# The first chunk of a decoder block, unit by unit: x and w_in interleaved, meta tokens loaded once, zeros multiplied before x lands

## What is computed

```python
u = rmsnorm(h, norm_attn_pre[l])          # h: [pad | 16 meta tokens | 256 rows of x]
z = u @ w_in[l]                           # w_in: (2048, 8448)
qa, ka, va, qb, kb, vb, ga, gb = jnp.split(z, SPLITS, axis=-1)
...
mix = jax.nn.sigmoid(ga) * (ya @ w_branch_a[l]) + jax.nn.sigmoid(gb) * (yb @ w_branch_b[l])
h = h + rmsnorm(mix @ w_out[l], norm_attn_post[l])
u = rmsnorm(h, norm_ff_pre[l])
f = jnp.square(jax.nn.relu(u @ w_ff1[l])) @ w_ff2[l]
h = h + rmsnorm(f, norm_ff_post[l])
```

## Time and profile before

| | |
|---|---|
| median of 3 runs | 1377.43 us (1377.38 to 1377.56) |
| profiled execution, its own time | 1377.66 us |
| its span, first to last instruction | 1375.9 us |
| PE busy (matmul) | 1356.5 us, 99% of the span |
| PE weight loads (beside the matmuls) | 1111.6 us, 81% |
| DVE busy | 759.3 us, 55% |
| ACT busy | 627.4 us, 46% |
| POOL busy | 51.5 us, 4% |
| first product of chunk 1 | starts at 36.79 us |

### The profile page before, as it was taken

How to read it: one execution, slowest core, us unless ns; L and a number is a source line. 1 busy time by engine, 2 the same in 40 slices (tenths; PEclk the granted TensorE clock), 3 DMA queues, 4 the chain that set the end, 5 groups by cost and what they waited for, 6 DMA issues and landing times.

```text
span 1375.9 us, 18595 instructions
## 1 busy us (share of the span) xinstructions
PE 1356.5 (99%) x6875; PEld 1111.6 (81%) x6875; DVE 759.3 (55%) x993; ACT 627.4 (46%) x916; POOL 51.5 (4%) x89
## 2 busy tenths in 40 slices
PE   6999999999999999999999999999999999999997
PEld 5876766777788888888988888888888888888886
DVE  5554544555565555555766545656556554556554
ACT  6544353455474444344554434443334443444442
POOL 1221120000000000000010000000000000000000
PEclk9999999999999999999999999999999999999999
DMA  8765454555546655775665656655566656666563
GB/s 226 224 178 143 143 163 132 152 150 163 155 154 191 190 184 188 238 247 178 203 215 185 197 179 204 186 189 193 184 200 185 189 192 195 190 187 193 187 197 107
DMA packets 130470, 253.07 MB, mean 184 GB/s; under 512 B 8548, under 2 KB 11040, under 8 KB 129933
## 3 DMA queue, kind: packets, MB, share of 16 engines
q1 hardware_dynamic: 126448, 241.28, 56.3%
q0 software_dynamic: 2192, 4.75, 1.8%
q10 hardware_dynamic: 1740, 5.88, 1.4%
HBM read 249.69 MB, written 2.17 MB: 183 GB/s over the span
## 4 chain that ended last, share of the span: by engine, by line
PE 98%; DVE 1%; DMA 1%; ACT 0%; issue 0%; SPq 0%; DVEq 0%; ACTq 0%
PE bank L1205 22%; PE bank L1207 21%; PE bank L1206 21%; PE bank L1491 16%; PE bank L1494 8%; PE bank L1223 1%; PE bank L1193 1%; PE bank L1515 1%; DMA xs<-in_x 1%; PE bank L1518 1%; PE bank L1318 1%; PE bank L1317 1%; PE bank L1362 0%; PE bank L1361 0%; PE bank L1351 0%; PE bank L1349 0%
## 5 line engine op out<-in xcount | busy, mean ns | idle before, releaser
L761 DVE TENSOR_TENSOR w_lo<-raw,w_hi 128x1024 fp32r<-128x1024 f32 (+1 forms) x456 | 550.0, 1214 | 440.4 <-ACT w_hi L385 439.7
L385 ACT ACTIVATE w_hi<-raw 128x1024 fp32r<-128x1024 f32 (+1 forms) x456 | 474.1, 1050 | 489.0 <-DMA raw<-in_w_ff 362.3
L1491 PE MATMUL bank<-f_hl,w_hi 128*128 128x512 f32 x960 | 260.1, 394 | 0.6 <-issue 0.6
L1205 PE MATMUL bank<-w_hi,u_hi 128*128 128x512 f32 (+1 forms) x544 | 216.3, 398 | 1.5 <-DVE w_lo L761 1.5
L1206 PE MATMUL bank<-w_lo,u_hi 128*128 128x512 f32 (+1 forms) x544 | 209.1, 384 | 0.0
L1207 PE MATMUL bank<-w_hi,u_lo 128*128 128x512 f32 (+1 forms) x544 | 209.1, 384 | 0.0
L1205 PE MATMUL bank<-w_hi,hid_hi 128*128 128x512 f32 x512 | 199.2, 389 | 0.0
L1206 PE MATMUL bank<-w_lo,hid_hi 128*128 128x512 f32 x512 | 199.2, 389 | 0.0
L1207 PE MATMUL bank<-w_hi,hid_lo 128*128 128x512 f32 x512 | 199.2, 389 | 0.0
L1491 PEld LDWEIGHTS bank<-f_hl,w_hi 128*128 128x128 f32 x960 | 165.0, 189 | 24.0 <-issue 1.0
L1494 PEld LDWEIGHTS bank<-f_hl,w_lo 128*128 128x128 f32 x960 | 145.3, 189 | 19.1
(11 more groups left out here) (201 smaller groups left out, 1019.5 us busy)
## 6 DMA issues: line engine op xcount, KB each, us to landing
raw<-in_w_ff SPq DMA_DIRECT2D x256, 512.0 KB, 3.7
raw<-in_w_in SPq DMA_DIRECT2D x128, 512.0 KB, 3.6
raw<-in_w_out SPq DMA_DIRECT2D x32, 512.0 KB, 4.6
raw<-in_w_branch_b SPq DMA_DIRECT2D x16, 512.0 KB, 3.7
raw<-in_w_branch_a SPq DMA_DIRECT2D x16, 512.0 KB, 3.7
xs<-in_x SPq DMA_DIRECT2D x4, 512.0 KB, 11.5
raw<-in_w_in SPq DMA_DIRECT2D x8, 256.0 KB, 12.6
bias<-bias_table POOLq DMA_DIRECT2D x8, 256.0 KB, 4.5
```

The lines of the kernel that those rows point to most:

```text
L385: act.activation(w_hi[:, u, :, 0:width], raw[:, u, :, 0:width], ACT.Copy).then_inc(hi_ready, 1)
L761: dve.tensor_tensor(w_lo[:, u, :, 0:width], raw[:, u, :, 0:width], w_hi[:, u, :, 0:width].bitcast(F32), ALU.subtract).then_inc(lo_ready, 1)
L1205: pe.matmul(ps[b][:, 0:width], hi_of(kt, b), wh, start=a, stop=False)
L1491: ins = pe.matmul(acc[g][:], w_hi[:, u, k, cols], f_hl[:, kt, :], start=kt == 0, stop=kt == KT - 1)
```

## The change

It replaces `START_ORDER` by one loop over the 8 units on SP, ACT and DVE: `keep_x(u)` and then the split of unit u. `turn_x(i)` now turns a quarter of what it did (4 transposes, one bank, 2 tiles of x), and PE does `turn_x(u + 2)` behind unit u. `turn_meta` moves behind unit 1, the first meta pair from behind unit 1 to behind unit 2. The meta tokens are loaded once, by ACT, after the first piece of x has landed; their squares are summed on 16 partitions, and a product with `spread_m`, a fourth 8 KB constant, puts the sum at the four places. `relx` and `buck` are loaded by ACT after its split of unit 2; POOL's small loads, now eight, wait until unit 7 has landed. DVE clears `rows` first of all, and PE multiplies it by itself, three times ahead of the gain's transposition and four times behind it.

```diff
         @block.gpsimd
-            pool.memset(xm[:], 0.0).then_inc(meta_zero, 1)
             pool.memset(meta_g[:], 0.0).then_inc(meta_zero, 1)
...
+            pool.wait_ge(landed[UNITS - 1], 16)
             for i, v in enumerate((lambda_q1, lambda_k1, lambda_q2, lambda_k2)):
...
+            pool.dma_start(spread_m[:], fold_t).then_inc(small_landed, 16)
...
         @block.scalar
-            act.wait_ge(meta_zero, 1)
-            act.dma_start(xm[0:META, :], meta_tokens).then_inc(xm_landed, 16)
-
             act.wait_ge(eps_set, 1)
             act.activation(sc[:, 1:2], eps, ACT.Copy)
-            act.wait_ge(rel_ones, 1)
-            act.dma_start(relx[0:N_BUCKETS, :], rel_bias).then_inc(rel_landed, 16)
-            act.dma_start(buck[:], buckets).then_inc(rel_landed, 16)
-            for g in range(1, MG):
-                act.dma_start(xm[g * MP:g * MP + META, :], meta_tokens).then_inc(xm_twice, 16)
+            act.wait_ge(x_landed[0], 16)
+            act.dma_start(xm[0:META, :], meta_tokens).then_inc(xm_landed, 16)
...
+            for u in range(UNITS):
+                keep_x(u)
+                split_hi(u, 0, 256)
+                if u == 2:
+                    act.wait_ge(rel_ones, 1)
+                    act.dma_start(relx[0:N_BUCKETS, :], rel_bias).then_inc(rel_landed, 16)
+                    act.dma_start(buck[:], buckets).then_inc(rel_landed, 16)
...
             act.activation(rstd, ssx, ACT.Sqrt, scale=1.0 / D, bias=eps).then_inc(stats, 1)
-            act.activation(rstdm, ssm, ACT.Sqrt, scale=1.0 / D, bias=eps).then_inc(stats, 1)
+            act.wait_ge(meta_spread, 1)
+            act.activation(rstdm, S1[:, 0:1], ACT.Sqrt, scale=1.0 / D, bias=eps).then_inc(stats, 1)
...
         @block.vector
+            dve.memset(rows[:], 0.0).then_inc(zeros_set, 1)
             dve.memset(eps, EPS).then_inc(eps_set, 1)
...
-                    link(dve.tensor_tensor_reduce(rows_m[:], xm[:, cols], xm[:, cols], 1.0, 0.0, ALU.mult,
-                                                  ALU.add, ss1[:, j:j + 1]))
+                    link(dve.tensor_tensor_reduce(rows_m[0:META, :], xm[0:META, cols], xm[0:META, cols], 1.0, 0.0,
+                                                  ALU.mult, ALU.add, ss1[0:META, j:j + 1]))
                 else:
-                    dve.tensor_reduce(ssm, ss1[:, 0:4], AX.X, ALU.add)
+                    dve.tensor_reduce(ssm[0:META, :], ss1[0:META, 0:4], AX.X, ALU.add).then_inc(meta_squared, 1)
                 split_ahead(0, u)
...
         @block.tensor
+            def stay_busy(n):
+
+                for _ in range(n):
+                    pe.matmul(bank[0][:, 0:256], rows[:, 0, 0:P], rows[:, 0, 0:256], start=True, stop=True)
+
+            pe.wait_ge(zeros_set, 1)
+            stay_busy(3)
             pe.wait_ge(consts_landed, 32)
             pe.transpose(bank[7][:, 0:KT], g_rows[:], ident[0:KT, 0:KT]).then_inc(gain_turned, 1)
...
+            stay_busy(4)
             turn_x(0)
-            turn_meta()
             turn_x(1)
...
-                    if c == 0 and u == 0:
+                    if c == 0 and u == 1:
+                        turn_meta()
+                    if c == 0 and u == 2:
                         pe.wait_ge(meta_scaled, 1)
-                    if c == 0 and u % 2:
-                        meta_pair(u // 2, [w_hi[:].bitcast(F32), w_lo[:].bitcast(F32)], 256, free=True)
+                    if c == 0 and u in (2, 3, 5, 7):
+                        meta_pair((u - 1) // 2, [w_hi[:].bitcast(F32), w_lo[:].bitcast(F32)], 256, free=True)
...
-                    if c == 0 and u < 2:
+                    if c == 0 and u + 2 < UNITS:
                         turn_x(u + 2)
                     if c == 0 and u == 6:
                         bias_table()
+                    if c == 0 and u == UNITS - 1:
+                        pe.wait_ge(meta_squared, 1)
+                        pe.wait_ge(small_landed, 8 * 16)
+                        pe.matmul(S1[:, 0:1], spread_m[:], ssm[0:META, :], start=True, stop=True)\
+                          .then_inc(meta_spread, 1)
```

More of the change, by code:

```diff
@@ L133, in hybrid_block @@
                  lambda_q2, lambda_k2, diff_norm, sinks, norm_attn_pre, norm_attn_post, w_ff1, w_ff2,
-                 norm_ff_pre, norm_ff_post, identity, fold, buckets, out):
+                 norm_ff_pre, norm_ff_post, identity, fold, fold_t, buckets, out):
     table = nc.dram_tensor("bias_table", (2, HA + HB, TAB), F32)
@@ L200, in hybrid_block @@
         fold_m = sb("fold_m", [P, META])
+        spread_m = sb("spread_m", [META, P])
         relx = sb("relx", [N_BUCKETS + 1, HA + HB])
@@ L223, in hybrid_block @@
         x_landed = [sem(f"x_landed{i}") for i in range(4)]
-        xm_landed, xm_twice, consts_landed = sem("xm_landed"), sem("xm_twice"), sem("consts_landed")
+        xm_landed, consts_landed, zeros_set = sem("xm_landed"), sem("consts_landed"), sem("zeros_set")
+        meta_squared, meta_spread = sem("meta_squared"), sem("meta_spread")
         rel_ones, rel_landed, small_landed = sem("rel_ones"), sem("rel_landed"), sem("small_landed")
@@ L297, in _ @@
             sp.dma_start(g_rows[:], norm_attn_pre[0].rearrange("(k p) -> k p", p=P)).then_inc(consts_landed, 16)
[L299 to L304, removed]
+            for u in range(UNITS):
+                if u % 2 == 0:
+                    cols = slice(u // 2 * CW, (u // 2 + 1) * CW)
+                    sp.dma_start(xs[:, :, cols], xf[:, :, cols]).then_inc(x_landed[u // 2], 16)
+                load(u, w_in, slice(u * 256, u * 256 + 256), slice(KB0, KB0 + 256), None, 256)
             for c in range(1, C_MIX):
@@ L368, in job_bias @@
                     pool.dma_start(bias[:, slot, 0, 0:META + SEQ], src).then_inc(bias_landed[slot], 16)
-            pool.wait_ge(small_landed, 7 * 16)
+            pool.wait_ge(small_landed, 8 * 16)
             pool.wait_ge(table_copied, 1)
@@ L785, in scale_meta @@
                 gains = g_col[:].rearrange("p (k a) -> p k a", a=1).broadcast_to([P, KT, META])
-                dve.wait_ge(meta_zero, 2)
+                dve.wait_ge(meta_zero, 1)
                 dve.tensor_tensor(meta_g[:, :, 0:META], bank[6][:, 0:KT * META].rearrange("p (k t) -> p k t", k=KT), gains,
@@ L798, in keep_x @@
                 last.then_inc(turned_lo, 1)
[L800 to L806, removed]
+            for u in range(UNITS):
+                keep_x(u)
+                split_lo(u, u + 1, 256)
+                if u == 2:
                     scale_meta()
             dve.wait_ge(xm_landed, 16)
-            dve.wait_ge(xm_twice, 16 * (MG - 1))
             for u in range(UNITS - LEAD, UNITS):
@@ L827, in _ @@
                .then_inc(norm, 1)
-            dve.wait_ge(small_landed, 7 * 16)
+            dve.wait_ge(small_landed, 8 * 16)
             for i in range(2):
@@ L1243, in turn_meta, with turn_x @@
                 ins.then_inc(meta_turned, 1)
-            def turn_x(j):
-                pe.wait_ge(x_landed[j], 16)
-                for i in (2 * j, 2 * j + 1):
-                    if i >= 4:
-                        pe.wait_ge(turned_lo, i - 3)
-                    turn4(bank[2 + i % 4], [xs[:, b, (2 * i + k) * P:(2 * i + k + 1) * P]
-                                            for k in range(2) for b in range(BLOCKS)]).then_inc(turned, 1)
+            def turn_x(i):
+                pe.wait_ge(x_landed[i // 2], 16)
+                if i >= 4:
+                    pe.wait_ge(turned_lo, i - 3)
+                turn4(bank[2 + i % 4], [xs[:, b, (2 * i + k) * P:(2 * i + k + 1) * P]
+                                        for k in range(2) for b in range(BLOCKS)]).then_inc(turned, 1)
             def bias_table():
@@ L1576 @@
     given["fold"] = np.concatenate([np.eye(MP, META, dtype=np.float32)] * MG)
+    given["fold_t"] = np.ascontiguousarray(given["fold"].T)
     given["buckets"] = bucket_table()
```

3 lines of the change are left out of this document (removed).

## The result

The changed kernel takes 1382.97 us (median of 5 runs, 1382.28 to 1383.32), the kernel before 1377.43 (1377.38 to 1377.70). The ratio is 1.0040, 95% interval 1.0029 to 1.0051: slower by 5.5 us. The profiled execution has a span of 1381.4 us, 5.5 more than before.

What follows compares the result with a forecast made beforehand. PE was taken to bound the kernel, so chunk 1's start sets the end. Later start +2.4 and clock fall +1.6 make +4.0 us on the median 1377.43: 1381.4 us, range 1379.2 to 1384.2.

Steps and rivals of the forecast that it cites:

- What bounds the kernel, and that later work gives nothing back: PE from 24.44 us: busy 1340.49 of 1341.56 us, so any shift of chunk 1's start moves the end equally.
- The transfers: Start, SP's queue: second piece of x lands by about 10 us instead of 12.4; costs or gives at most 0.8 us.
- The start of PE: Before the first turn of x: clear 0.9 us, PE starts at about 1.8, seven zero products raise the clock.
- T: Time when PE first turns x: 6.7 to 8.6 us, taken as 7.0, against 6.71 before.
- Chunk 0: PE at the higher clock: unit 0 at 10.1, last turn ends 26.65, chunk 0 ends 32.2, 4.6 us sooner than 36.79.
- the stall ahead of unit 5: PE in chunk 0: only there too little work lies between turn and unit, so it waits 0.7 us.
- The new wait: Ahead of chunk 1: PE idles 7 us for the meta squares' sum; chunk 1 starts at 39.15, +2.4 us.
- The clock: Start of chunk 1: the idle time drops the clock to 1.2 GHz, costing 1.6 us (1.4 to 2.0).
- that the sum is early: Rival, end of chunk 0: sum ready before 32.2, chunk 1 starts at once; -4.4 us, 1373.0; chance 0.06.
- that zeros don't count: Rival, start: zeros don't raise the clock, or data come late; T = 8.6, +3.2 on top, up to 1384.6; chance 0.10.
- the short wait: Rival, ahead of chunk 1: wait short or without clock fall; +1.0 to +2.7 us, 1378.4 to 1380.1; chance 0.20.

Runs made afterwards that it cites:

- e9: Kernel before, with POOL's small loads behind unit 7's landing, relx and buck issued behind ACT's unit 0 split, three meta copies behind unit 1: 1375.94 us, ratio 0.9981.
- e2: e1 with the turn of K and V moved from behind chunk 1's third unit to behind its seventh: 1374.30 us, ratio 0.9968.
- e1: Changed kernel, with DVE's four meta squares and their sum moved into chunk 0 behind units 3 to 6: 1383.66 us, ratio 1.0034.
- e3: Changed kernel, with 14 more zero products ahead of the spread product and DVE's bias table copy behind it: 1381.55 us, ratio 1.0024.
- e4: Changed kernel without the seven zero products and the clear of rows: 1383.97 us, ratio 1.0038.
- e7: Kernel before, with POOL's small loads behind unit 7's landing; relx, buck and three meta copies behind ACT's unit 3 split: 1381.17 us, ratio 1.0021.
- e5: e1 with ACT's squares of x moved too, one behind the split of each unit of chunk 0: 1375.25 us, ratio 0.9981.
- e6: e2 with ACT's squares of x moved too, one behind the split of each unit of chunk 0: 1374.18 us, ratio 0.9975.
- e10: e2 with two zero products instead of four behind the gain's turn: 1374.85 us, ratio 0.9976.
- e8: Kernel before, with the clear of rows and the seven zero products alone: 1379.08 us, ratio 1.0004.

## Why the prediction was right

The likeliest value was 1381.4 us, in a range of 1379.2 to 1384.2; 1382.97 lies in it, 1.6 us above the likeliest. The mechanism was right in every step that the 5.5 us are made of; what was off were sizes.

**What bounds the kernel, and that later work gives nothing back.** Right: the start of chunk 1 and its clock, 3.85 + 1.7, account for the 5.5 us.

**The transfers.** Right: SP's queue moved 1.90 MB from 9 to 15 us, and PE turned the second piece of x without a wait at 12.51, the third and fourth too, and the meta tokens at 14.47. e9 adds that in the kernel before this part alone gives 2 us, of which the prediction had spoken as 0.8 at most for the new order.

**The start of PE.** The clear took 0.91 us (0.9 was taken), but DVE began at 1.03 instead of 0.82. T was 7.72, within 6.7 to 8.6, for 7.0: the clock rose about 4.5 us after the first zero product and not 3.04, so that the second group ran 1.5 of its 2.65 us at 1.2 GHz (by its length: an instruction took 0.48 us in the first group, half of that at the fast clock). This is the largest miss, 0.7 us, and its size is chance: the same instructions gave 7.18 in e2 and 7.98 in e1.

**Chunk 0.** Unit 0 came 3.28 us behind T (3.1), the stall ahead of unit 5 was 0.66 us (0.7), the last turn ended 20.1 us behind T (19.65), chunk 0 at 33.5 (32.2; 0.7 of it from T).

**The new wait.** Right in place, in cause and in length: 6.57 us for L811 (7 was taken), ACT's chain of 10.74 us from the first square (10.78). e1 and e2 show that this wait and the one hidden behind it at the turn of K and V are the whole of the loss. That second wait the prediction did not have; in the changed kernel it costs nothing, because the first covers it.

**The clock.** 1.7 us for 1.6. From the end of the sum to chunk 1's first product it took 0.56 us for 0.15, since the spread product ran at the low clock as well: 0.51 us, and 0.31 at the full clock in e3. That makes 5.5 against 4.0: the terms were all on the low side, by 0.7 (T), 0.2 (unit 0), 0.2 (the rest of chunk 0), 0.4 (the spread product) and 0.1 (the clock). That the sum still lies in the range owes something to the width that was given to T.

**The rivals.** That the sum is early fell (the first square at 29.34 and not before 21.4), that zeros don't count fell with e3 and e4, and so did the short wait, since the wait was 6.57 us long and the clock fell in it.

## What to carry to other kernels

A new wait on the engine that bounds the kernel is priced by following its releaser backwards through the program order of every engine: here one small sum stood, by old habit, behind four splits and eight squares on two engines, and cost more than the whole rebuilt stage gave. When a stage is made faster, look up what the next stage takes from the other engines and when that will be ready; removing the first wait alone (e1) gave nothing, moving the taker as well (e2) made a kernel 3.5 us faster than the one before. And the idle times of 6.6 and 5.9 us on TensorE cost twice here, once for themselves and about 2 and 3 us more for the clock behind them; that of 1.81 us in e7 cost 1.7 us more.

## What was not expected of the hardware

The time after which the clock moved was not the same from place to place, nor from one execution to the next. Up to the first turn of x, PE has the same instructions in the changed kernel, e1, e2, e3, e5 and e6, and never waits from the first zero product at 2.00 on. The turn starts at 7.72 in the changed kernel; the earliest and latest but for e6 (7.15) are those of e2 and e1:

```profile
7.18 1.04 PE L1184 MATMUL bank<-ident,xs 128*128 128x128 f32 x8
```

```profile
7.98 1.04 PE L1184 MATMUL bank<-ident,xs 128*128 128x128 f32 x8
```

By the length of the second group of zeros, the clock rose about 3.5 us after the first zero product in e2, 4.5 in the changed kernel and 5.1 in e1; in e10 it was about 3.6. These are estimates from the spacing, because the granted clock in the profile reads 1.00 there throughout. In the kernel before it rose about 3 us after 12.43, in e1, after the wait at the turn of K and V, only 6.6 us after PE was back at work at 48.51 (a mean of 0.96 from 55 to 56).

It fell 2.9 us after PE's last product at the end of the kernel before, 3.9 us into the wait of the changed kernel, 3.0 us into that of e8 (a mean of 0.84 from 16 to 17) and 2.3 us into that of e1 (0.92 from 44 to 45). In e7 it fell at about 1015.3 (a mean of 0.63 in the stretch 1015 to 1016), when PE had stood idle 1.81 us and was back at work since 1014.57, and it came back in the stretch 1018 to 1019. So the expectation of e5, that the clock does not fall in a wait of 1.6 us, held there, where the wait was 0.5 us, but is no rule. A margin of an idle time against the fall, or of work towards the rise, cannot be read from one run.
